# Expert weights of a mixture-of-experts stage loaded as half matrices into a ring of sixteen 1 MB buffers instead of whole matrices into eight of 2 MB

## The reference

```python
def hier_moe(u, wg, bg, we, be, w_gate, w_up, w_down):   # w_gate, w_up: 64 x 1024 x 512; w_down: 64 x 512 x 1024
    # each token gets two experts of one group, with gates
    ...
    # for every block of tokens of one expert e:
    #   hidden = silu(x @ w_gate[e]) * (x @ w_up[e])       (tokens x 512)
    #   y      = hidden @ w_down[e]                        (tokens x 1024)
    # out[token] = sum over its two experts of gate * y
```

## Time and profile before

| | us |
|---|---|
| median of 3 runs | 3783.04 |
| lowest and highest run | 3777.04, 3783.94 |
| profiled execution, its own time | 3787.08 |
| span of the profiled execution, first to last instruction | 3785.2 |

### The profile page before, as it was taken

One profiled execution on the slowest core, in us unless ns is written; L12 is line 12 of the kernel. 1 busy time (PEld: TensorE's weight loads), 2 busy tenths in 40 slices (PEclk: granted clock), 3 DMA queues, 4 the chain that ended last, 5 costly groups with the idle time before them and its releaser, 6 DMA issues. The chain is left out here.

```text
span 3785.2 us, 26001 instructions
## 1 busy us (share of the span) xinstructions
PE 2876.2 (76%) x9024; PEld 1313.4 (35%) x9024; DVE 1369.1 (36%) x3223; ACT 552.9 (15%) x1332; POOL 662.6 (18%) x592
## 2 busy tenths in 40 slices
PE   6956884777777777857657989888987787677767
PEld 3432542223333333323254433433443333233223
DVE  1033112000000000012192011566677667766774
ACT  1021100000000000001211010222222222222222
POOL 0000002000000000000120000244343444444433
PEclk9956586899999999978868999999998889888889
DMA  2100005999999999961001212599999999999998
GB/s 96 43 21 0 0 27 234 428 427 427 427 427 427 426 427 427 427 267 34 19 1 61 74 53 78 216 410 398 416 395 400 389 408 406 405 393 412 404 402 333
DMA packets 137673, 1047.11 MB, mean 277 GB/s; under 512 B 20929, under 2 KB 21713, under 8 KB 46929
## 3 DMA queue, kind: packets, MB, share of 16 engines
q0 software_dynamic: 81024, 562.08, 36.5%
q1 hardware_dynamic: 51920, 466.74, 30.1%
q10 hardware_dynamic: 4608, 16.78, 1.1%
HBM read 1020.35 MB, written 25.19 MB: 276 GB/s over the span
## 5 line engine op out<-in xcount | busy, mean ns | idle before, releaser
L1598 PE MATMUL psum<-peer_ring,peer_diag 128*128 128x512 f32 x2048 | 969.6, 632 | 289.9 <-ACT peer_diag L1639 289.6
L1524 POOL DMA_INDIRECT peer_ring<-in_peer_uv,peer_pick x512 | 569.4, 1112 | 1217.6 <-PE psum L1598 747.1
L1731 DVE CUSTOM_DVE_ANT_0 peer_ring<-peer_ring,sb_rows 128x1024 f32<-128x1024 f32 x512 | 618.4, 1224 | 372.6 <-DMA peer_ring<-in_peer_uv,peer_pick 370.8
L1598 PEld LDWEIGHTS psum<-peer_ring,peer_diag 128*128 128x128 f32 x2048 | 408.0, 203 | 843.7 <-issue 483.2
L928 PE MATMUL psum<-moe_w,moe_xT 128*64 128x512 f32 x2048 | 519.0, 664 | 169.3 <-DMA moe_w<-in_w_up 124.3
L974 DVE TENSOR_TENSOR moe_hd<-psum,moe_sg 128x512 f32<-128x512 f32 x32 | 22.1, 692 | 941.3 <-ACT moe_sg L956 941.3
L928 PEld LDWEIGHTS psum<-moe_w,moe_xT 128*64 128x64 f32 x2048 | 181.5, 153 | 505.8 <-issue 504.0
L232 PE MATMUL psum<-mix_xn,sb_tiles 128*128 128x512 f32 x640 | 280.4, 601 | 31.0 <-PEq L1198 20.1
L949 PE MATMUL psum<-moe_w,moe_hT 128*64 128x512 f32 x1024 | 230.0, 601 | 38.4 <-DVE moe_hT L979 33.6
L1001 POOL DMA_INDIRECT sb_tiles<-token_rows,ffn_block_tok x32 | 30.4, 949 | 906.2 <-PE psum L919 905.7
L232 PEld LDWEIGHTS psum<-mix_xn,sb_tiles 128*128 128x128 f32 x640 | 123.5, 193 | 188.0 <-issue 188.0
(11 more groups left out here) (343 smaller groups left out, 2280.0 us busy)
## 6 DMA issues: line engine op xcount, KB each, us to landing
moe_w<-in_w_gate SPq DMA_DIRECT2D x64, 2048.0 KB, 30.2
moe_w<-in_w_up SPq DMA_DIRECT2D x64, 2048.0 KB, 33.2
moe_w<-in_w_down SPq DMA_DIRECT2D x64, 2048.0 KB, 31.0
expert_rows<-sb_tiles ACTq DMA_DIRECT2D x32, 512.0 KB, 10.2
sb_tiles<-in_w_in2b SPq DMA_DIRECT2D x28, 512.0 KB, 3.6
sb_tiles<-in_w_out SPq DMA_DIRECT2D x16, 512.0 KB, 3.5
sb_tiles<-in_w_query SPq DMA_DIRECT2D x16, 512.0 KB, 5.1
peer_ring<-in_peer_uv,peer_pick POOLq DMA_INDIRECT x512
```

The costliest lines, as they stand in the source:

```text
L1524: pool.indirect_dma_start(out=ring[:, slot], out_offset=None, in_=A["peer_uv"], in_offset=bass.IndirectOffsetOnAxis(ap=pick[:, i, j:j + 1] ...
L1598: last = nc.tensor.matmul(ps[:, 2 * i + c], diag[:, b % DIAGS, x], ring[:, slot, D + 512 * c:D + 512 * (c + 1)], start=False, stop=end, sk ...
L1731: dve.tensor_tensor_reduce(ring[:, n % RING, 0:D], ring[:, n % RING, 0:D], hr[:, i], 1.0, 0.0, ALU.mult, ALU.add, dots[:, i, j + x:j + x + ...
```

## The change

A load brings half a matrix: the first or the second 8 KB of each partition's 16 KB (`PART` elements), which for gate and up are k 0 to 3 and k 4 to 7, for down k 0 and 1, then k 2 and 3. The ring has sixteen buffers of 8 KB per partition, of the same total size. The order of the 384 loads is, for each kind: first part of both experts, second part of both experts. PE waits for a part's two buffers before that part's matmuls, and increments `used` after each part, so that the counts of `used` run twice as fast. In `down` the loop over parts stands outside that over the column blocks b, so the two blocks alternate by part. The overflow block is changed in the same manner.

```diff
@@ def experts
-    F, RING, PAIRS = D_EXPERT, 8, N_EXPERTS // 2
+    F, RING, PAIRS = D_EXPERT, 16, N_EXPERTS // 2
...
+    PART = KD * F // 2
-    uses = PAIRS * 6
+    uses = PAIRS * 12
-        wr = st.sb("w", [P, RING, KD * F])
+        wr = st.sb("w", [P, RING, PART])
...
-        def weights(slot, k, width, c0, n):
-            return wr[:, slot, k * width + c0:k * width + c0 + n]
+        def weights(slots, half, k, width, c0, n):
+            part = k * width // PART
+            at = k * width + c0 - part * PART
+            return wr[:, slots[2 * part + half], at:at + n]
...
         def into(pe, kind, bank, u, slots, waits):
-            for half in range(2):
-                pe.wait_ge(landed[slots[half]], waits[half])
-            for k in range(KD):
+            for part in range(2):
                 for half in range(2):
-                    r = slice(SLOTS * half, SLOTS * half + SLOTS)
-                    last = nc.tensor.matmul(ps[r, bank], xT[:, u, k, r], weights(slots[half], k, F, 0, F),
-                                            start=k == 0, stop=k == KD - 1)
-            last.then_inc(used[kind], 1)
+                    pe.wait_ge(landed[slots[2 * part + half]], waits[2 * part + half])
+                for k in range(part * KD // 2, (part + 1) * KD // 2):
+                    for half in range(2):
+                        r = slice(SLOTS * half, SLOTS * half + SLOTS)
+                        last = nc.tensor.matmul(ps[r, bank], xT[:, u, k, r], weights(slots, half, k, F, 0, F),
+                                                start=k == 0, stop=k == KD - 1)
+                last.then_inc(used[kind], 1)
...
         def down(pe, n, slots, waits):
-            for half in range(2):
-                pe.wait_ge(landed[slots[half]], waits[half])
             pe.wait_ge(h_ready, n + 1)
             pe.wait_ge(yo_ready, 2 * n)
-            for b in range(2):
-                for k in range(KE):
-                    for half in range(2):
-                        r = slice(SLOTS * half, SLOTS * half + SLOTS)
-                        last = nc.tensor.matmul(ps[r, 6 + b], hT[:, k, r], weights(slots[half], k, D, b * 512, 512),
-                                                start=k == 0, stop=k == KE - 1)
-            last.then_inc(used[DOWN], 1)
+            for part in range(2):
+                for half in range(2):
+                    pe.wait_ge(landed[slots[2 * part + half]], waits[2 * part + half])
+                for b in range(2):
+                    for k in range(part * KE // 2, (part + 1) * KE // 2):
+                        for half in range(2):
+                            r = slice(SLOTS * half, SLOTS * half + SLOTS)
+                            last = nc.tensor.matmul(ps[r, 6 + b], hT[:, k, r], weights(slots, half, k, D, b * 512, 512),
+                                                    start=k == 0, stop=k == KE - 1)
+                last.then_inc(used[DOWN], 1)
...
         def slots_of(q, kind):
-            return [(6 * q + 2 * kind + half) % RING for half in range(2)]
+            return [(12 * q + 4 * kind + x) % RING for x in range(4)]
...
                     if n >= RING:
-                        sp.wait_ge(used[(n - RING) % 6 // 2], (n - RING) // 6 + 1)
-                    sp.dma_start(wr[:, n % RING], source[n % 6 // 2][2 * (n // 6) + n % 2]).then_inc(landed[n % RING], 16)
+                        sp.wait_ge(used[(n - RING) % 12 // 4], (n - RING) // 12 * 2 + (n - RING) % 4 // 2 + 1)
+                    part = n % 4 // 2
+                    sp.dma_start(wr[:, n % RING], source[n % 12 // 4][2 * (n // 12) + n % 2, :, part * PART:(part + 1) * PART]
+                                 ).then_inc(landed[n % RING], 16)
```

More of the change, by code:

```diff
@@ L940, in down @@
         def down(pe, n, slots, waits):
-            for half in range(2):
-                pe.wait_ge(landed[slots[half]], waits[half])
             pe.wait_ge(h_ready, n + 1)
             pe.wait_ge(yo_ready, 2 * n)
-            for b in range(2):
-                for k in range(KE):
-                    for half in range(2):
-                        r = slice(SLOTS * half, SLOTS * half + SLOTS)
-                        last = nc.tensor.matmul(ps[r, 6 + b], hT[:, k, r], weights(slots[half], k, D, b * 512, 512),
-                                                start=k == 0, stop=k == KE - 1)
-            last.then_inc(used[DOWN], 1)
+            for part in range(2):
[8 more added lines that the diff above has]
+                last.then_inc(used[DOWN], 1)
         def activate(act, n):
-            act.wait_ge(used[UP], n + 1)
+            act.wait_ge(used[UP], n * 2 + 2)
             act.wait_ge(hd_ready, n)
@@ L958, in result_out @@
         def result_out(act, row, u, n, wait):
-            act.wait_ge(used[DOWN], n + 1)
+            act.wait_ge(used[DOWN], n * 2 + 2)
             act.wait_ge(stored[u], wait)
@@ L967, in tokens_out @@
             dve.wait_ge(turned, n + 1)
-            dve.wait_ge(used[UP], seen)
+            dve.wait_ge(used[UP], seen * 2)
             dve.tensor_copy(xT[:, u], ps[:, 0:2].rearrange("p b (k s) -> p (b k) s", s=S2)).then_inc(x_ready, 1)
@@ L977, in hidden_out @@
             dve.wait_ge(h_turned, n + 1)
-            dve.wait_ge(used[DOWN], n)
+            dve.wait_ge(used[DOWN], n * 2)
             dve.tensor_copy(hT[:], ps[:, 4].rearrange("p (k s) -> p k s", s=S2)).then_inc(h_ready, 1)
         def slots_of(q, kind):
-            return [(6 * q + 2 * kind + half) % RING for half in range(2)]
+            return [(12 * q + 4 * kind + x) % RING for x in range(4)]
         def waits_of(q, kind):
-            return [16 * ((6 * q + 2 * kind + half) // RING + 1) for half in range(2)]
+            return [16 * ((12 * q + 4 * kind + x) // RING + 1) for x in range(4)]
         with nc.Block() as block:
@@ L1056, in body @@
                         for kind in range(3):
-                            sp.wait_ge(used[kind], b + PAIRS)
-                            sp.dma_start(wr[:, 2 * kind + half], source[kind][e]).then_inc(landed[2 * kind + half], 16)
+                            sp.wait_ge(used[kind], b * 2 + 2 * PAIRS)
+                            for part in range(2):
+                                slot = 4 * kind + 2 * part + half
+                                sp.dma_start(wr[:, slot], source[kind][e, :, part * PART:(part + 1) * PART]).then_inc(landed[slot], 16)
                 spilled(sp, body)
@@ L1075, in body @@
                 def body(b):
-                    waits = [(b + EACH + 1) * 16] * 2
+                    waits = [(b + EACH + 1) * 16] * 4
                     turn_tokens(pe, 0, b + PAIRS, (b + PAIRS // 2 + 1) * 16)
@@ L1079, in body @@
                     pe.wait_ge(hd_ready, b + PAIRS)
-                    into(pe, GATE, 2, 0, (0, 1), waits)
-                    into(pe, UP, 3, 0, (2, 3), waits)
+                    into(pe, GATE, 2, 0, (0, 1, 2, 3), waits)
+                    into(pe, UP, 3, 0, (4, 5, 6, 7), waits)
                     turn_hidden(pe, b + PAIRS)
-                    down(pe, b + PAIRS, (4, 5), waits)
+                    down(pe, b + PAIRS, (8, 9, 10, 11), waits)
                 spilled(pe, body)
```

## The result

The changed kernel takes 3796.49 us (median of 9 runs, 3785.97 to 3801.61), the kernel before 3785.73 us (median of 9 runs in the same sets): 10.8 us slower, a ratio of 1.0027 with a 95% interval of 1.0015 to 1.0039. The profiled execution took 3798.13 us (span 3796.3), against 3787.08 (3785.2).

The account below looks back on a forecast made before the run. The prediction took the expert stage's DMA engines, without idle time, as the bound; packets +13.5 and the stage's end -6.1 summed to +7.4 us on 3783.04, giving 3790.4 us, range 3778 to 3808.

Parts of the forecast that it names:

- The bound of 7.6 us: Whole kernel: about 0.2%, the least difference a measurement can tell; chances faster 0.06, same 0.42, slower 0.52.
- What bounds the kernel: Expert stage: the sixteen DMA engines have no free time (share 1.01, 427 GB/s), while PE has 172.7 us of slack.
- Packets, +13.5 us: Expert stage's weight loads: 49,152 packets of 8 KB replace 24,576 of 16 KB, at 8.8 ns per packet; range 9.4 to 17.7.
- The gather's price: Rival for weight loads: 8 KB packets cost 322.5 ns as in the last stage's gathers, 3820.8 us in all; chance 0.10.
- the estimate worked out from the Trainium skill: Weight loads' packet term: about 4.7 ns per packet, making 7.2 us; the forecast used the trace's 8.8 ns.
- Issues and loads, nothing: SP in the expert stage: 192 more issues at 428 ns, 82 us, are covered by the transfers.
- Latency of loads of 1 MB: Rival in the expert stage: 2.2 us more per load, not overlapped, costs 430 us (4213 in all); chance 0.02.
- Finer waits, nothing within the stage: PE in the expert stage: earlier starts and releases gain nothing; total waiting about as long, in twice as many or more.
- The end, -6.1 us: End of the expert stage: last up-projection in two pieces, no slow clock, last down matmul 6.1 us earlier; range 3.5 to 7.7.
- The queue on SP: SP in the expert stage: it mostly waits, and a load takes 428 ns to issue.

Follow-up runs that it names:

- e4_waits_first: Changed kernel, but PE waits for all four half matrices of a matrix pair before its first matmul; ratio to the kernel before 1.0027, stage 1063.2 us.
- e1_pad8: Kernel before, still 192 loads, with a 64-byte gap in each buffer row, so packets are 8 KB instead of 16 KB; 3802.55 us, ratio 1.0031.
- e12_ring12: Changed kernel with a ring of twelve buffers instead of sixteen; 3796.47 us, ratio to the kernel before 1.0031.
- e5_tail2: Kernel before, with only the last pair's six matrices loaded and used as halves; 3785.57 us, ratio 0.9988.
- e6_tail4: Kernel before, with only the last pair's matrices loaded and used as quarters; 3783.16 us, ratio 0.9991.
- e9_joined: Kernel before, with gate and up of an expert side by side in one 4096 KB load, 32 KB packets; 3819.65 us, ratio 1.0077.
- e2_pad4: Kernel before, still 192 loads, with gaps in each buffer row giving four 4 KB packets per partition; 3832.56 us, ratio 1.0108.
- e8_order: Changed kernel with loads reordered: both halves of the first expert, then both of the second; 3801.53 us, ratio to the kernel before 1.0035.
- e7_quarters: The change taken to quarters of a matrix: 768 loads of 512 KB, ring of 32, 4 KB packets; ratio to the kernel before 1.0108.

## Why the prediction was right

The forecast was 3790.4 us, +7.4 against the median shown; measured were +10.8 (5.7 to 14.8 by the interval) and +9.4 in the stage of the profiled executions. The time itself, 3796.49, lies 6.1 above the forecast; 2.7 of these come from the kernel before, whose median is 3785.73 over nine runs instead of 3783.04. The bound of 7.6 us, nearly an even choice in the chances, lies inside the interval, so the runs don't settle on which side of it the kernel is. Step by step:

**What bounds the kernel.** Right. The share stayed at 1.01, and a faster PE ended nothing sooner: e4_waits_first has 17.6 us more of PE work in the 900 than the changed kernel, and its last up part started at the same 1044.3.

**Packets, +13.5 us.** Right in mechanism, and the term that was mis-sized. The price of a packet was read from rows in which one packet of 4 bytes comes with every eight of data, as in the changed kernel, so this term stands for all that its transfers cost more. That was 15.6 us (16.5 by the landing), 2 to 3 us over the forecast and inside its 9.4 to 17.7. e1_pad8 measured 13.6, but for the data packets alone: it has one small packet to sixteen. That 8.8 ns came out so near to 8.9 and 9.0 is in part luck. A packet of 8 KB, with its share of the small ones, took 315.1 ns by the queue row instead of 312.6, which alone would make the term (49,152 x 315.1 - 24,576 x 616.4) / 16 = 21.2 us. But the forecast also kept the overlap of packets as it was, and it grew, from 100.8 to 101.3% of the engines' time. That is about 5 us of the stage and gives most of the rest back. So 9 ns is what a packet adds to the stage's time with this overlap, not what it takes on its engine. The gather's price of 43.9 us was three times too high. By the estimate worked out from the Trainium skill (DMA: Bandwidth & Descriptors, "Why small descriptors are slow") this term would have been 7.2 us; e1_pad8's 13.6 is nearly twice that, and decides.

**Issues and loads, nothing.** Right for SP: its issue time is covered (e12_ring12: medians of 0.43 to 0.46 us instead of 2.1 to 2.5, the landing doesn't move). But the transfers of the changed kernel end 2.9 us later than in e1_pad8 with the same data packets in half the loads. 1.7 us of that are the small packets of the 192 loads more; the packet term above has them in its price. The rest are slightly longer data packets, for a reason that stays open.

**Latency of loads of 1 MB.** It doesn't show. The Trainium skill (DMA: Bandwidth & Descriptors, "Measured") has 341 GB/s for 1 MB, in DMAs issued from GpSimd; that is far from the 420 of loads of 1024 KB and from the 410 of loads of 512 KB in SP's queue. The rule beside it asks for 1 MiB or more. The halves just meet that, so the forecast went too far in writing that the section asks for larger ones.

**Finer waits, nothing within the stage.** Right in time, wrong in a detail: I expected PE's total wait to stay; it grew from 172.7 to 210.0 us. The longer stage and PE's shorter own work (27 us in 900) can account for that. With the same bytes, matmuls and rate, e4_waits_first has a mean clock of 0.92 instead of 0.96, so the higher clock comes from the finer waits.

**The end, -6.1 us.** Measured -6.2 from the landing of up's weights (19.9 to 13.8), and e4_waits_first shows that it belongs to the waits: 5.1 us by the stage, the rest being the clock, which came back sooner there than before. Two pieces and a clock of 1.00, as forecast.

**The queue on SP.** I wrote that SP mostly waits, with issues of 428 ns. Not so: it sat in issues of 2.1 us. It cost nothing.

## What to carry to other kernels

Where the DMA engines have no idle time, as in this stage, its length is the time of its packets, plus what stands behind the last landing. Each row of 16 KB that was cut in two added about 9 ns on one of 16 engines, and each load 16 small packets of 9 ns; splitting loads bought nothing in the middle. The gain of finer loads lay at the end of the stream, behind the last landing, so split only the last ones (e5_tail2, e6_tail4). When loads are joined for larger packets, look first at what then holds the buffers: in e9_joined the queue ran dry.

## What the runs showed that I had not expected

SP's queue can fill, and in these runs that goes by packets rather than by loads. With sixteen loads of 128 packets allowed in flight, an issue takes 2.1 us in the median and up to 9.2; with twelve 0.43 to 0.46, up to 4.0. With eight loads of 256 packets (e1_pad8) it takes up to 16.5 us, with eight of 512 (e2_pad4) 4.9 to 6.2 in the median; with eight of 128, as before, never more than 0.71. In the one pair that differs in this alone, the changed kernel and e12_ring12, the data landed at the same time.

A row of 32 KB goes as one packet.

Waits in more and shorter pieces raised PE's mean granted clock in the stage: 0.96 in the changed kernel and 0.97 in e12_ring12 against 0.92 in e4_waits_first and e8_order, all at 420 GB/s; with quarters (e7_quarters) it was 1.00.
